# Output projections that wait for their inputs part by part, with the first two tiles cut in two pieces

## What is computed

```
h = rms_norm(x)
y = concat(attention(h), bidirectional_recurrence(h), gated_convolution(h))   # 512 + 256 + 256 wide
x = x + y @ w_out                       # output projection
x = x + mlp(rms_norm(x))
```

```
h = rms_norm_2(x);  proj = h @ w_in
branch = einsum("bsnc,ncd->bsnd", [y_nsa, y_sb, y_gla, y_fox], w_branch)
mixed = sum(sigmoid(gate_logits + b_gate) * branch, axis=2)      # over the four branches
x = x + mixed @ w_out                   # output projection
x = x + square(relu(rms_norm_2(x) @ w_ff1)) @ w_ff2
```

## Time and profile before

| | |
|---|---|
| runs shown | 4065.33, 4067.52, 4071.44 us, median 4067.52 us |
| the profiled execution's own time | 4068.66 us |
| its span in the trace | 4066.5 us |
| granted TensorE clock over the span | 0.955 of full |
| busy, PE | 3733.8 us, 92% of the span |
| busy, DVE | 2072.0 us, 51% |
| busy, ACT | 1319.8 us, 32% |
| busy, POOL | 1283.6 us, 32% |

### The profile page before, as it was taken

The page is one execution under the profiler, slowest core; times in us unless marked ns, Lnnn a source line. Parts: engine busy times, 40 slices in busy tenths (PEclk is TensorE's granted clock), DMA queues, the critical chain, the costliest instruction groups (busy, mean ns, idle before and its releaser), DMA issues. The chain is left out here.

```text
span 4066.5 us, 46227 instructions
## 1 busy us (share of the span) xinstructions
PE 3733.8 (92%) x17918; PEld 2842.7 (70%) x17918; DVE 2072.0 (51%) x2990; ACT 1319.8 (32%) x2225; POOL 1283.6 (32%) x522
## 2 busy tenths in 40 slices
PE   7888999887899979999999989998899999989997
PEld 5555888665578857676777668886657777668885
DVE  4886555398654533533263465443352255345453
ACT  5344111343421121434333421112254433332112
POOL 2202444330144423132323244442113232224442
PEclk9889999997999989999999999999999999899998
DMA  3101333220023232121212123333212122113322
GB/s 111 52 11 42 99 94 93 74 63 16 26 94 94 93 108 86 36 64 57 81 55 73 47 78 94 98 93 112 59 32 78 58 72 68 57 59 95 97 93 67
DMA packets 80145, 292.58 MB, mean 72 GB/s; under 512 B 9616, under 2 KB 10928, under 8 KB 79408
## 3 DMA queue, kind: packets, MB, share of 16 engines
q1 hardware_dynamic: 77136, 278.49, 22.0%
q10 hardware_dynamic: 2784, 11.03, 0.8%
HBM read 285.30 MB, written 2.10 MB: 71 GB/s over the span
## 5 line engine op out<-in xcount | busy, mean ns | idle before, releaser
L207 POOL TENSOR_TENSOR w_lo<-w_raw,w_hi 128x1024 fp32r<-128x1024 f32 x518 | 1283.4, 2478 | 2736.7 <-ACT w_hi L193 2736.6
L193 ACT ACTIVATE w_hi<-w_raw 128x1024 fp32r<-128x1024 f32 x518 | 549.1, 1060 | 1828.7 <-PE acc L244 1757.8
L242 PE MATMUL acc<-hH,w_hi 128*128 128x512 f32 x1840 | 778.5, 423 | 130.9 <-DVE hL L305 70.1
L244 PE MATMUL acc<-hL,w_hi 128*128 128x512 f32 x1840 | 732.0, 398 | 0.0
L243 PE MATMUL acc<-hH,w_lo 128*128 128x512 f32 x1840 | 731.7, 398 | 0.0
L242 PEld LDWEIGHTS acc<-hH,w_hi 128*128 128x128 f32 x1840 | 355.5, 193 | 232.1 <-issue 111.7
L275 DVE TENSOR_TENSOR xT<-acc,xT 128x512 f32<-128x512 f32 x160 | 110.7, 692 | 639.5 <-PE acc L244 639.5
L242 PE MATMUL acc<-H,w_hi 128*128 128x512 f32 x1024 | 405.8, 396 | 5.9 <-issue 4.2
L243 PEld LDWEIGHTS acc<-hH,w_lo 128*128 128x128 f32 x1840 | 355.4, 193 | 76.5 <-issue 12.0
L244 PEld LDWEIGHTS acc<-hL,w_hi 128*128 128x128 f32 x1840 | 353.7, 192 | 78.0
L242 PE MATMUL acc<-midH,w_hi 128*128 128x512 f32 x1024 | 403.7, 394 | 4.2 <-issue 4.2
(11 more groups left out here) (325 smaller groups left out, 4578.5 us busy)
## 6 DMA issues: line engine op xcount, KB each, us to landing
w_raw<-in_stream SPq DMA_DIRECT2D x518, 512.0 KB, 3.5
cw<-in_cmpw ACTq DMA_DIRECT2D x2, 2048.0 KB, 7.9
mixed<-in_cmpw ACTq DMA_DIRECT2D x2, 2048.0 KB, 14.0
x_tok<-in_x SPq DMA_DIRECT2D x1, 2048.0 KB, 9.0
out<-f_tok SPq DMA_DIRECT2D x4, 512.0 KB, 2.6
stack<-Z ACTq DMA_DIRECT2D x8, 128.0 KB, 3.6
stack<-Z ACTq DMA_DIRECT2D x8, 127.8 KB, 3.7
masks_f<-in_masks SPq DMA_DIRECT2D x1, 960.0 KB, 10.8
```

The lines of the kernel that those rows point to most:

```text
L193: act.activation(w_hi[:, u % WB, 0:w], w_raw[:, u % 2, 0:w], ACT.Copy).then_inc(hi_split, 1)
L207: pool.tensor_tensor(w_lo[:, u % WB, 0:w], w_raw[:, u % 2, 0:w], w_hi[:, u % WB, 0:w], ALU.subtract)\
L242: pe.matmul(acc[n % 2][:, :], wh, H[:, k, :], start=(k == 0), stop=False)
L244: last = pe.matmul(acc[n % 2][:, :], wh, Lo[:, k, :], start=False, stop=(k == nk - 1))
```

## The change

In the first block the eight tiles of the output projection no longer wait for the end of stage `att` on ACT and DVE. PE waits for the convolution's reads of the two PSUM banks, and then input tile by input tile. In the second block the wait for the end of `mix3` goes from PE and from ACT, and DVE splits each tile of `mixed` right behind its add, counted by `out_split`. In both, the first two output tiles are made in two pieces (`some`): tile 0 and tile 1 with the inputs named first, then tile 0 and tile 1 with the rest. The first block takes inputs 4, 5, 0, 1, 2 and then 3, 6, 7; the second 0 to 3 and then 4 to 7. Tiles 2 to 7 are made as before.

```diff
+            def some(self, tile, ks, ready, begin, end):
+                u, t, n = self.tiles[tile]
+                _, nk, ntile, _ = self.units[u]
+                H, Lo = self.operands(nk)
+                if begin:
+                    pe.wait_ge(lo_split, u + 1)
+                    if n >= 2:
+                        pe.wait_ge(acc_free[n % 2], n // 2)
+                for j, k in enumerate(ks):
+                    ready(k)
+                    c = k * ntile * P + t * P
+                    wh, wl = w_hi[:, u % WB, c:c + P], w_lo[:, u % WB, c:c + P]
+                    pe.matmul(acc[n % 2][:, :], wh, H[:, k, :], start=(begin and j == 0), stop=False)
+                    pe.matmul(acc[n % 2][:, :], wl, H[:, k, :], start=False, stop=False)
+                    last = pe.matmul(acc[n % 2][:, :], wh, Lo[:, k, :], start=False, stop=(end and j == len(ks) - 1))
+                if end:
+                    last.then_inc(acc_ready[n % 2], 1)
...
-        def out_pe(units, sq):
+        def out_pe(units, early, late, ready):
             out_tiles = Group(units, "out")
+            for ks in (early, late):
+                for tile in range(2):
+                    out_tiles.some(tile, ks, ready, ks is early, ks is late)
+            del out_tiles.tiles[0:2]
             out_tiles.products()
             finish(pe, "out")
...
@@ first block, PE @@
                         att.pe(side=conv_pe)
                         finish(pe, "att")
-                        after(pe, stages, "att", act_finished, dve_finished)
-                        out_pe(units, pair)
+                        pe.wait_ge(conv_mean, 2)
+                        pe.wait_ge(conv_rstd, 1)
+
+                        def out_ready(k):
+                            if k < 4:
+                                pe.wait_ge(att.o_free, k + 1)
+                            if k >= 6:
+                                pe.wait_ge(conv_split, k - 5)
+                        out_pe(units, [4, 5, 0, 1, 2], [3, 6, 7], out_ready)
...
@@ first block, DVE @@
-                            split_dve(hH[:, 6 + j, :], hL[:, 6 + j, :], conv_c[:, j, :])
+                            link(dve, dve.tensor_copy(hH[:, 6 + j, :], conv_c[:, j, :]))
+                            dve.tensor_tensor(hL[:, 6 + j, :], conv_c[:, j, :], hH[:, 6 + j, :], ALU.subtract)\
+                                .then_inc(conv_split, 1)
...
@@ second block, PE @@
                         finish(pe, "mix3")
-                        after(pe, stages, "mix3", dve_finished)
-                        out_pe(units, pair)
+                        out_pe(units, [0, 1, 2, 3], [4, 5, 6, 7], lambda k: pe.wait_ge(out_split, k + 1))
...
@@ second block, ACT @@
                         finish(act, "mix3")
-                        after(act, stages, "mix3", dve_finished)
                         out_act(units, V2["norm_ff"], yt, pair)
...
@@ second block, DVE @@
                         def take_last(i, a, free, value):
                             dve.wait_ge(gate_opened, 3 * NK + i + 1)
                             add_branch(3, i, Z0[:, i, :], a, free, value)
+                            dve.wait_ge(branch_mixed, 3 * NK + i + 1)
+                            link(dve, dve.tensor_copy(hH[:, i, :], mixed[:, i, :]))
+                            dve.tensor_tensor(hL[:, i, :], mixed[:, i, :], hH[:, i, :], ALU.subtract).then_inc(out_split, 1)
                         Group(units, "mix3").evacuate(take_last)
-
-
-                        for k in range(NK):
-                            split_dve(hH[:, k, :], hL[:, k, :], mixed[:, k, :])
                         finish(dve, "mix3")
```

More of the change, by code:

```diff
@@ L140, in program @@
         sq_ready, sq_added, sq_summed, rstd_ready = sem("sq_ready"), sem("sq_added"), sem("sq_summed"), sem("rstd_ready")
+        out_split, conv_split = sem("out_split"), sem("conv_split")
         x_scaled, h_split, mid_ready = sem("x_scaled"), sem("h_split"), sem("mid_ready")
```

## The result

The changed kernel takes 4032.55 us (median of 4 runs, 4029.56 to 4037.94) where the kernel before takes 4067.9 (4 runs): a ratio of 0.9915, 95% interval 0.9902 to 0.9927. That is 35.4 us faster; 41.5 were forecast, and the time lies inside the range of 4020 to 4036. The profiled execution took 4029.56 us for a span of 4027.4, so 39.1 us less than the profiled one before.

What follows compares the result with a forecast made beforehand. PE was taken to bound the kernel, with 36.9 us of drain waits at four output projections. Gains of 13.5 us (first block) and 28.0 (second) sum to 41.5, so 4067.52 becomes 4026.0 us, range 4020 to 4036.

Steps and rivals of the forecast that it cites:

- What bounds the kernel: Whole kernel: PE, busy 92%; six waits for DVE's drain cost 40.1 us, 36.9 of it at four output projections.
- First block, 13.5 us: Last attention matmul to DVE's read of output tile 1: 18.16 and 18.21 us become 11.42, if the clock stays up.
- The clock's share: First output tile behind PE's idle time: slow clock costs 1.7 us per layer in first block, 2.8 in second.
- Second block without contention, 15.6 us per layer: Last `mix3` matmul to DVE's read of output tile 1: 27.04 us becomes 11.42, gaining 15.6 per layer.
- What the moved splits cost: Second block's `mix3`: POOL holds DVE's casts and adds at the shared port, making PE lose 1.6 us per layer.
- POOL takes the port in every gap of DVE: Rival, chance 0.11: each POOL turn in `mix3` costs DVE its whole 2.4 us, 3 us more per layer; 4032.
- One sign: In `mix3`, DVE's last multiply comes about 1 us later against the first one (2347.84 - 2327.76).
- The two pieces cover it with 1.6 us to spare: Second block's projection: last split ends near 2354.6, input 7 is wanted after 33 further matmuls, near 2356.2.
- Edits at nothing: Both blocks: new PE semaphore waits, ACT's earlier table load, bunched weight copies and DVE's later order cost nothing.
- PE finds another wait: Rival, chance 0.04: PE waits for weights in place of the drain; 4047 if half the gain goes, 4067.5 if all.
- the rival of a slower kernel: Chance 0.02: DVE keeps the port in `mix3`, PE stops for `w_lo`, 9 to 12 us per layer; could reach 4076.
- DVE is not held by POOL: Rival, chance 0.08: phases in `mix3` fall luckily, 3.2 us more gain; 4022.8.

Runs made afterwards that it cites:

- the filler: Kernel before, with 22 and 55 unread fp32r matmuls in PE's idle time ahead of the first and second block's output projections; 4060.61 us.
- the two repeats: The changed kernel run again unaltered, beside the kernel before: 4032.74 us and 4035.41 us.
- even splits: Changed kernel, but DVE splits tiles 0 to 3 behind adds 0, 2, 4, 6 of `mix3`, the others behind the last add; 4028.42 us, again 4026.92.
- even splits and whole tiles: Changed kernel with splits behind every second `mix3` add, the last four behind the last add, and the first two output tiles made whole; 4035.56 us.

## Why the prediction was right, and where it was off

- *What bounds the kernel.* Right: PE's waits for the drain were the places, and the four stretches hold all of the difference between the two profiled runs but 1.1 us.
- *First block, 13.5 us.* Measured 13.2. The clock did not fall (1.00 in the window). The missing 0.3 us is the boundary: PE stands 0.41 us there, where 0.26 were taken from a boundary with nothing to wait for the earlier trace rows.
- *The clock's share.* The prediction read 1.7 and 2.8 us per layer from the windows; the filler shows 1.6 and 2.65.
- *Second block without contention, 15.6 us per layer.* Right: without contention the stretch is 46.07 - 30.48 = 15.6 us shorter.
- *"What the moved splits cost", 1.6 us per layer.* The mechanism is right, the size is not: 3.18. The layout by hand put no hold between the multiplies of tiles 4 and 5 (2.9 and 2.7 us late), so its third turn of POOL fell behind tile 4's split. In the trace POOL entered between tile 4's add and its cast. So tile 5 was taken 4.6 us behind the end of its last matmul (2324.50) instead of 2.7, and PE lost 0.15, 0.95 and 1.79 us ahead of tiles 4, 6 and 7, counted from one matmul's start to the next beyond the usual 0.23, instead of 0.8 and 0.2 ahead of 6 and 7. In return nothing was lost at the boundary, where 0.6 had been put. The rival "POOL takes the port in every gap of DVE" holds for this one turn, and the 3.18 us lie between its price (1.6 + 3 = 4.6) and the forecast's. POOL does not win each time: its second turn is shown with 2.79 us instead of 2.4 to 2.5, because DVE's subtraction (2319.83 to 2320.52) was already running. One sign also failed by this: the last multiply was to come about 1 us later against the first one, and came 23.36 us behind it (2334.10 - 2310.74) instead of 19.06, 4.3 us later.
- *"The two pieces cover it with 1.6 us to spare."* Its claim on the last split holds: it ended 27.57 us behind the first multiply instead of 26.8, and PE never waited at `out_split`. But it gave the pieces a role that they don't have here, in the first block above all ("with that cover gone (all inputs in order) PE would wait as before"). Whole tiles with the same waits are as good in the first block and 0.4 us worse per layer in the second. The gain is that of the waits part by part; the pieces pay (2.7 us per layer) only where the splits come late.
- *Edits at nothing.* Right: no wait for `w_lo` came in, which "PE finds another wait" and the rival of a slower kernel both needed. "DVE is not held by POOL" is refuted.
- *The median.* 41.5 us were forecast and 35.4 measured. Of the 6.1 us between, 3.2 are the contention and 0.3 the boundary. The other 2.6 lie outside the four stretches: these give 38.0 us, the medians 35.4, and in the comparisons of the two repeats 37.4 and 32.7. The prediction counted what follows as the same work and put nothing there. The rest of the program took 3936.9 us in the profiled run of the changed kernel and 3945.0 and 3944.0 in its two repeats. The same stretches as in the last two lines of the windows above, in the first repeat:
```profile
355.92:1071.29 715.37, 656.11 (x3150) 493.36 (x3148) 451.17 (x550) 232.66 (x368) 231.25 (x92) 0.94 0.22 68
2775.00:3578.34 803.34, 757.04 (x3858) 562.83 (x3857) 339.85 (x677) 302.20 (x601) 221.27 (x92) 0.96 0.20 62
```
  Each is 3.1 to 3.3 us longer with the same work (a few records are missing) and has 2.3 to 3.1 us more busy time of PE. It goes with the clock: over the whole span that was 0.959 in the profiled run and 0.957 in both repeats, and 0.002 of 4030 us is 8 us. Other kernels show the same steps (3943.4 with whole tiles, 3938.5 to 3939.8 with even splits, 3946.2 with even splits and whole tiles).
  Part of the gain does seem to be given back there. In all eleven comparisons of this study the medians give less than the stretches, by 0.4 to 5.4 us. If in every run the stretches are as long as in the profiled ones, the rest takes 3937.9 us in the mean of the kernel before (35 runs) and 3941.5 in the changed one (13 runs, single runs of either spread over 3934 to 3945). With the first block's half alone it is 3938.4 (10 runs), with the second's alone 3940.9 (4 runs). The profile of the kernel before has 3938.0, near its mean, and that of the changed kernel 3936.9 has its lowest. By these means some 3 to 4 us come back as time outside the change, most of it with the second block's half. Why the clock is low more often there is not shown.

## What to carry to other kernels

Where the bounding engine waits for a whole stage's end, let it wait for its inputs one by one first; in the first block here that alone brought all of the gain, and cutting tiles in pieces pays only if an input is still late in natural order. Work moved under a stage must be laid out against every other user of its port, gap by gap: halving the splits inside the stage kept POOL's turns off them and won 2.9 us per layer back. PE's idle time cost more than its own length here (8.5 us of clock on 36.9), so fill the wait with harmless matmuls once to measure what the clock adds. And read a gain of this size both in its stretches, which repeat within 0.1 us, and in the medians, since the stretches don't see what changes elsewhere.

## What the runs showed of the hardware that was not expected

- A gap of 0.03 us between two DVE instructions, the second of which waits for the first's semaphore (an add until 2325.87, a cast from 2325.90), was enough for a POOL subtraction to take the port, in both layers; the cast then took 2.53 us instead of 0.43. The Trainium skill, in "SBUF — State Buffer", section "SBUF: two separate sides", describes an exclusive lock for the whole instruction; the trace agrees, and shows that the lock is not kept from one instruction to the next. Whether POOL had been waiting is not shown: its record begins 0.13 us before the add ends, but at 2.41 us is no longer than usual.
- A 128 x 512 matmul of plain fp32 operands made two records and cost 0.845 us (18.6 us for 22), one of fp32r operands 0.227, both at a granted clock of 1.00.
- At the places of this change, 5.35 us of PE's idle time cost 1.6 us more through the clock, and 13.08 us cost 2.65.
